# Start addresses of the moving operands in a hybrid encoder layer: SBUF regions reordered, and the moving side shifted by 24 bytes

## What is computed

```
x = x + 0.5 * (silu(h @ w1_gate) * (h @ w1_up)) @ w1_down      h = rmsnorm(x), hidden width 2816
z = rmsnorm(x) @ w_in                                          -> attention group and mLSTM group
x = x + concat(attention, rmsnorm(sigmoid(o) * mlstm)) @ w_out
x = x + 0.5 * (silu(h @ w2_gate) * (h @ w2_up)) @ w2_down      h = rmsnorm(x)
x = rmsnorm(x)
```

## Time and profile before

| | |
|---|---|
| runs | 1953.38, 1958.89 and 1961.13 us, median 1958.89 us |
| profiled execution | span 1956.0 us, 2.9 us below the median of the runs; no other time of that execution is recorded |
| TensorE matmuls (PE) | 1935.7 us busy, 99% of the span, 14627 matmuls |
| TensorE weight loads (PEld) | 1892.8 us busy, 97% |
| VectorE (DVE) | 1299.8 us, 66% |
| ScalarE (ACT) | 783.1 us, 40% |
| GpSimd (POOL) | 1064.0 us, 54% |
| granted TensorE clock | 9 tenths or more in all 40 slices, mean 0.998 |

### The profile page before, as it was taken

The page is one execution under the profiler, slowest core; times in us unless marked ns, Lnnn a source line. Parts: engine busy times, 40 slices in busy tenths (PEclk is TensorE's granted clock), DMA queues, the critical chain, the costliest instruction groups (busy, mean ns, idle before and its releaser), DMA issues.

```text
span 1956.0 us, 39225 instructions
## 1 busy us (share of the span) xinstructions
PE 1935.7 (99%) x14627; PEld 1892.8 (97%) x14627; DVE 1299.8 (66%) x1882; ACT 783.1 (40%) x1595; POOL 1064.0 (54%) x958
## 2 busy tenths in 40 slices
PE   8999999999999999999999999999999999999998
PEld 7999999999999999999998999999999999999997
DVE  6776777767467678864445655867777667656674
ACT  6433333333443345733335542433333333344343
POOL 3277776775777641321222442247767776676770
PEclk9999999999999999999999999999999999999999
DMA  8135445444995540343332735214454444498552
GB/s 269 45 112 175 142 156 179 136 131 145 310 324 179 169 109 9 114 126 91 97 103 62 208 98 117 78 64 136 162 178 132 132 154 163 148 363 270 167 156 103
DMA packets 226846, 293.88 MB, mean 150 GB/s; under 512 B 16616, under 2 KB 158472, under 8 KB 226736
## 3 DMA queue, kind: packets, MB, share of 16 engines
q1 hardware_dynamic: 219040, 272.76, 43.7%
q0 software_dynamic: 7696, 19.63, 3.2%
HBM read 198.07 MB, written 94.21 MB: 149 GB/s over the span
## 4 chain that ended last, share of the span: by engine, by line
PE 93%; POOL 2%; DVE 2%; DMA 2%; issue 1%; ACT 1%; SPq 0%; ACTq 0%; POOLq 0%
PE bank L282 28%; PE bank L284 28%; PE bank L283 28%; PE bank L2574 1%; PE bank L2593 1%; PE bank L2584 1%; POOL HA L1378 1%; DMA WRAW<-in_w_down 1%; DMA XIN<-in_x_prompt 1%; PE bank L2505 0%; PE bank L1325 0%; PE bank L1323 0%; PE bank L1324 0%; PE bank L1319 0%; PE bank L2685 0%
## 5 line engine op out<-in xcount | busy, mean ns | idle before, releaser
L282 PE MATMUL bank<-HA,HW 128*128 128x272 f32 x1120 | 322.7, 288 | 0.5 <-POOL HA L1378 0.5
L284 PE MATMUL bank<-HA,HW 128*128 128x272 f32 x1120 | 322.8, 288 | 0.0
L283 PE MATMUL bank<-HA,HW 128*128 128x272 f32 x1120 | 321.6, 287 | 0.0
L1372 DVE SCALAR_TENSOR_TENSOR HW<-WRAW,HW 128x512 fp32r<-128x512 f32 x140 | 223.2, 1633 | 107.2 <-ACT HW L1367 106.9
L1378 POOL TENSOR_TENSOR HA<-ARAW,HA 128x544 fp32r<-128x544 f32 x140 | 219.5, 1583 | 106.1 <-ACT HA L1366 105.9
L282 PE MATMUL bank<-HH,WGH 128*128 128x362 f32 (+2 forms) x784 | 255.1, 325 | 1.2 <-issue 1.2
L283 PE MATMUL bank<-HL,WGH 128*128 128x362 f32 (+2 forms) x784 | 246.5, 314 | 0.0
L284 PE MATMUL bank<-HH,WGL 128*128 128x362 f32 (+2 forms) x784 | 246.2, 314 | 0.0
L282 PE MATMUL bank<-FC,WR 128*128 128x272 f32 x768 | 222.1, 289 | 0.4 <-issue 0.2
L284 PE MATMUL bank<-FC,WR 128*128 128x272 f32 x768 | 221.7, 289 | 0.0
L283 PE MATMUL bank<-FC,WR 128*128 128x272 f32 x768 | 221.1, 288 | 0.0
(11 more groups left out here) (384 smaller groups left out, 5704.0 us busy)
## 6 DMA issues: line engine op xcount, KB each, us to landing
asp<-SA SPq DMA_DIRECT2D x44, 544.0 KB, 3.4
RAWG<-in_w_gate SPq DMA_DIRECT2D x22, 1024.0 KB, 6.5
RAWU<-in_w_up SPq DMA_DIRECT2D x22, 1024.0 KB, 6.4
tsp<-TT SPq DMA_DIRECT2D x40, 544.0 KB, 6.7
ARAW<-tsp SPq DMA_DIRECT2D x80, 272.0 KB, 3.3
WS<-in_w_down SPq DMA_DIRECT2D x20, 1024.0 KB, 8.7
wsp<-WS SPq DMA_DIRECT2D x20, 1024.0 KB, 8.5
WRAW<-wsp SPq DMA_DIRECT2D x80, 256.0 KB, 4.3
```

What stands on the lines that cost most here:

```text
L282: nc.tensor.matmul(bank[:, 0:w], w_hi, rhs_hi, start=first, stop=False)
L283: nc.tensor.matmul(bank[:, 0:w], w_hi, rhs_lo, start=False, stop=False)
L284: return nc.tensor.matmul(bank[:, 0:w], w_lo, rhs_hi, start=False, stop=last)
L1372: nc.vector.scalar_tensor_tensor(out=HW[f][h][:, 1], in0=WRAW[r][:, :], scalar=0.5, in1=HW[f][h][:, 0].bitcast(F32), op0=ALU.mult, op1=ALU ...
```

## The change

The regions of weights, raw data, scratch and constants come first, then 24 bytes of padding (region "moving"), then x, hh, hl and a. All four therefore start 24 bytes past a multiple of 64 and everything in them moves by 24 bytes modulo 64; the regions wg, raw, d, t and c keep starts at multiples of 64. Inside the six slots of the down tiles the weight tile HW is put 8 bytes further, and the second slot of each of two pairs as well. `place` gets a way to put a tensor at an offset that is no multiple of 32: it allocates from the multiple below and returns a view. No instruction, semaphore, shape or order is changed.

```diff
@@ -48,6 +48,8 @@
 WRING = 5
+CONSTANTS = 5568
+MOVING = 24
 GROUPS = [(0, 1, 2), (3, 4, 5), (6, 7, 8)]
@@ -65,7 +67,14 @@
         def place(name, shape, dtype, offset):
-            return nc.alloc_sbuf_tensor_at(name, shape, dtype, offset=base + offset)
+            lead, size = offset % 32, 1
+            if lead == 0:
+                return nc.alloc_sbuf_tensor_at(name, shape, dtype, offset=base + offset)
+            for n in shape[1:]:
+                size *= n
+            flat = nc.alloc_sbuf_tensor_at(name, [shape[0], lead // 4 + size], dtype, offset=base + offset - lead)
+            names = [f"d{i}" for i in range(len(shape) - 1)]
+            return flat[:, lead // 4:lead // 4 + size].rearrange(f"p ({' '.join(names)}) -> p {' '.join(names)}", **dict(zip(names, shape[1:])))
@@ -76,16 +85,17 @@
+        rWG = region("wg", 2 * 4 * 4096)
+        rRAW = region("raw", 4 * 4096)
+        rD = region("d", 3 * 8192)
+        rT = region("t", 8 * NW * 4)
+        rC = region("c", CONSTANTS)
+        region("moving", MOVING)
         rX = region("x", KT * T * 4)
         rHH = region("hh", KT * T * 4)
         rHL = region("hl", KT * T * 4)
         rA = region("a", 4 * T * 4)
-        rWG = region("wg", 2 * 4 * 4096)
-        rRAW = region("raw", 4 * 4096)
-        rD = region("d", 3 * 8192)
-        rT = region("t", 8 * NW * 4)
-        rC = region("c", 0)
-        assert base + rC < nc.sbuf_usable_end
+        assert base + at["end"] <= nc.sbuf_usable_end
@@ -127,9 +137,9 @@
-        slot_at = [[rHL, rHL + 8448, rHL + 17408, rHL + 17408 + 8448, o_ + 17408, o_ + 26112] for o_ in (rX, rHH)]
+        slot_at = [[rHL, rHL + 8456, rHL + 17408, rHL + 17408 + 8456, o_ + 17408, o_ + 26112] for o_ in (rX, rHH)]
         HA = [[place(f"HA{f}{h}", [P, 2, 2, HT], F32R, slot_at[f][h]) for h in range(SLOTS)] for f in range(2)]
-        HW = [[place(f"HW{f}{h}", [P, 2, 512], F32R, slot_at[f][h] + 4352) for h in range(SLOTS)] for f in range(2)]
+        HW = [[place(f"HW{f}{h}", [P, 2, 512], F32R, slot_at[f][h] + 4352 + 8) for h in range(SLOTS)] for f in range(2)]
```

More of the change, by code:

```diff
@@ L215, in build @@
         RMB = small("RMB", [NB + 1, LH])
-        assert base + small_at <= nc.sbuf_usable_end
+        assert small_at <= rC + CONSTANTS
         BANK = [ctx.enter_context(nc.psum_tensor(f"bank{i}", [P, 512], F32)) for i in range(8)]
```

## The result

The changed kernel takes 1972.41 us (median of 4 runs, 1971.93 to 1973.12) against 1958.54 us beside it: a ratio of 1.0072, 95% interval 1.0059 to 1.0084. It is slower by 14 us, where 22 us less was forecast; 1972 lies above the range's upper end of 1969. The profiled execution spans 1971.6 us, 15.6 us more than the one before.

What follows compares the result with a forecast made beforehand. The prediction took the distance between TensorE's matmul starts as the bound; 16.5 + 3.1 + 1.2 + 2.5 - 1.0 = 22.3 us saved gave 1933.7 for the profiled execution, a median of 1937 us, range 1912 to 1969.

Steps and rivals of the forecast that it cites:

- What bounds the kernel: Whole kernel: TensorE's matmuls fill 99% of the span, so time is matmul count times the distance between starts.
- The third tile's lesson carried to 272 columns: w_in's third tile, 24 past 64, has 10.6 ns above its columns; the 272-wide products were to get the same, 123.9 ns.
- Gate and up: Gate and up products, 7488 matmuls at 2.2 ns less each: 16.5 us saved, from 27.0 saved to 4.5 lost.
- Down: Down products, 3360 matmuls, two thirds gaining 1.4 ns each: 3.1 us saved, from 9.4 saved to 4.7 lost.
- w_out: Products of w_out, 768 matmuls from 125.5 ns: 1.2 us saved, from 2.3 saved to 0.9 lost.
- the bound of 126.7: Highest distance in ns allowed for gate and up, taken from a w_out tile, meaning no gain: 4.5 us lost.
- w_in: Three row tiles of w_in and the last pair's product: first 2.5 us saved, second 1.9 saved, third 1.9 lost; sum 2.5 saved.
- Other engines at nothing: VectorE, ScalarE, GpSimd and DMA at shifted addresses: no cost, and hidden under PE's 99%.
- GpSimd at the start of down: Start of each down stage: PE cannot outrun GpSimd's deliveries, taking 1 us off the gain, 2 us with the larger gain.
- its case of more: Rival: all 272-wide products find the low pattern, 122.5 ns or a step below: 39 us saved, 1920 us, chance 0.20.
- The remainder is not what matters: Rival: the third w_in tile is cheap by accident of width and start; 272-wide products stay at 125 to 126.7 ns, 1961 us, chance 0.22.
- One more line: Rival: each 272-wide read crosses 69 lines of 16 bytes, not 68, costing 1.7 ns per matmul: 1978 us, chance 0.13.

Runs made afterwards that it cites:

- e1: Changed kernel with padding 0 in place of 24 and the slots as before, so only the new region order: 1949.25 us, 0.9957 of the kernel before.
- e7: Changed kernel with 28 bytes of padding and slots laid out anew, every HA at remainder 12 modulo 16, HW at multiples of 64: 1945.95 us, 0.9939 of before.
- e4: Changed kernel with 28 bytes of padding in place of 24, nothing else: 1944.93 us, 0.9930 of the kernel before.
- m1: Matmul chains alone, computation left out, sweeping the moving start over 256 bytes, some with shifted weights: means 124.3 to 127.6 ns by remainder modulo 16 at 272 columns.
- m3: Matmul chains alone at 362 and 364 columns over all starts, and 272 with narrower weight tiles: 362-column means 164.0 to 166.8 ns by remainder modulo 16.
- m2: Matmul chains alone with the low part 64 or 128 bytes further on, as in the kernel, each twice: means 124.3 to 127.7 ns by remainder modulo 16.
- e2: Changed kernel with regions d, t and c put behind the moving ones, operands 24 modulo 256 from the weights: 1969.1 us, 1.0054 of the kernel before.
- e6: Changed kernel with 20 bytes of padding in place of 24: 1977.91 us, 1.0102 of the kernel before.
- e8: Changed kernel with 40 bytes of padding in place of 24: 1974.09 us, 1.0083 of the kernel before.
- e9: Changed kernel with 16 bytes of padding in place of 24: 1957.3 us, 0.9996 of the kernel before.
- e3: Changed kernel with d, t and c behind the moving regions, no padding, slots as before, operands 0 modulo 256 from the weights: 1959.1 us, 1.0005 of before.
- e5: Changed kernel with 28 bytes of padding, HW 84 bytes further in the slots in place of 8, and slots 1 and 3 moved: 1947.08 us, 0.9941 of before.

## Why the prediction was wrong

**What bounds the kernel: held.** PE's 99% and its matmul distance decide; no other engine took part in the result, and the sum of distances gives the span within 1.5 us.

**The third tile's lesson carried to 272 columns: the step that failed.** The prediction takes "the third tile's mean of 10.6 ns on top" as that of a 24-byte start. The low level was not that of the start modulo 64: in e1 the same tile, with the same 24 bytes and width and 64 bytes more to the weights, has 165.1 ns, 14.3 on top. Chains with its addresses ran at 163.3 and 166.7 ns, 12.5 and 15.9 on top, and the second tile after holds 160.0 ns for three units and then leaves it, from another address. 364 columns 24 past have 15.0 on top, in the chains and in the first tile after; 272 columns have 14.2 in the changed kernel. Gate and up: 16.5 us saved were forecast, 10.1 lost. Down: 3.1 saved, 3.9 lost. w_out: 1.2 saved, 1.0 lost. Gate and up lost more than the 4.5 us set as its worst: 127.5 ns lies outside the bound of 126.7, since the rows of before held only aligned starts at 272 columns.

**The order of the regions: a term left out.** The part-by-part sum speaks of remainders modulo 64 alone. The new order moves the operands by 64 bytes against the weights, and that is worth -9 us in e1, the one good thing in the change. The gain of e1 is luck for this forecast, since the prediction has no term for it. The two together make the result: 9 gained, 23 lost.

**w_in: one tile in three.** The third tile lost 2.0 us where 1.9 was said; it now lies at 176 modulo 256 from the weights, as the second did before, so taking over the second's distance was right. The first stayed at 166.7 ns, where 2.5 us were to be saved, and the second at 164.4 where 1.9 were.

**Other engines at nothing: held for the time**, 1658 ns for the subtraction; the low parts of the down stage became 8% faster, which is told at the end.

**GpSimd at the start of down: not reached** by the changed kernel; e7 loses some 2 us there.

**A slip in the sums.** With a third of the down products at 1.4 ns either way, the most that down could save is 2240 x 2.8 + 1120 x 1.4 = 7.8 us. The prediction has 9.4, all 3360 at 2.8, and its case of more is 1.6 us too fast by it.

**The rivals.** "The remainder is not what matters" had the right doubt about the third tile and the wrong conclusion: the remainder matters, modulo 16, and against the change. "One more line" gave 1978 us, the sign and nearly the size, by a mechanism that e4 excludes. Its own sign spoke against it in the changed kernel already: the first tile of w_in crosses one line more than before, too, and stayed at 166.7 ns. The Trainium skill, "SBUF — State Buffer", section "Specifications (TRN2)", has the 16-byte lines and a penalty for each crossing. The remainder modulo 16 does order the means of the chains; the penalty for crossings doesn't: a start at remainder 12, with one line more than an aligned one, is the cheapest of all, 124.3 against 125.0 ns in the chains.

**What stays open.** Why remainder 12 is cheap and 4 dear; why the distance to the weights acts in steps of 64, and by how much in steps of 16; whether the weights' own remainder matters, since in gate and up they never moved modulo 256 (with the weights 8 bytes on, m1's four chains at remainder 0 and four at 8 have nearly the same mean, 125.5 and 125.8 ns); what puts the same addresses now into one level, now into the next. No run here separates the read of the moving rows from that of the weights inside one matmul.

## What to carry to other kernels

When a kernel is a row of back-to-back matmuls, treat the start address of the moving operand as a setting to be measured: eight bytes moved this one by 33 us out of 1958. Measure it as chains with the kernel's own widths and its own pattern of operands, since a level read at one width did not hold at the next, and give each edit its position against the weights as well as its own. And when a change of layout does two things, price each of them.

## What the runs showed that was not expected

**A grid.** The means of the chains gather at 160.0, 163.3, 166.7 and 170 ns at 362 columns, and at 123.3, 126.7 and 130.0 at 272, steps of 3.3 ns: in m1 and m3 a little over half of them lie within 0.2 ns of one of these. The rest, and most of m2's, lie in between.

**Low parts that became faster.** The groups of VectorE's and GpSimd's low parts by line, before and then after (count, busy us, mean ns, idle before):
```profile
L1372 DVE SCALAR_TENSOR_TENSOR HW<-WRAW,HW 128x512 fp32r<-128x512 f32 x140 | 223.2, 1633 | 107.2 <-ACT HW L1367 106.9
L1378 POOL TENSOR_TENSOR HA<-ARAW,HA 128x544 fp32r<-128x544 f32 x140 | 219.5, 1583 | 106.1 <-ACT HA L1366 105.9
```
```profile
L1382 DVE SCALAR_TENSOR_TENSOR HW<-WRAW,HW 128x512 fp32r<-128x512 f32 x140 | 205.6, 1506 | 118.7 <-ACT HW L1377 118.4
L1388 POOL TENSOR_TENSOR HA<-ARAW,HA 128x544 fp32r<-128x544 f32 x140 | 200.2, 1446 | 126.5 <-ACT HA L1376 126.0
```
8% less for the same operations. e2, e6 and e8 have it too (1484 to 1512 and 1441 to 1445 ns); e4 and e9 half of it (1578 and 1560, 1524 and 1516); e1, e3, e5 and e7 nothing (1632 to 1656, 1593 to 1603). All that gain have HW 8 bytes on from its old place in the slot, so it goes with the layout: e9's PE is as fast as before's and its low parts are faster. PE's speed may have a share in it all the same, since the four kernels with the whole 8% are the four with the slowest PE. Under a PE at 99% it is worth nothing; the cause was not tried.
